# Leaving a root on the residual: post norms that multiply instead of divide, in a fused three-block transformer kernel

## The reference, cut to what matters

```
def rms_norm(x, g):
    y = xf * lax.rsqrt(jnp.mean(xf * xf, axis=-1, keepdims=True) + RMS_EPS)
    return (y * g.astype(jnp.float32)).astype(x.dtype)
...
h = h + rms_norm(mixer(rms_norm(h, mix_pre)), mix_post)
h = h + rms_norm(swiglu_ffn(rms_norm(h, ffn_pre)), ffn_post)
```

## Time and profile before

| | |
|---|---|
| median of 3 runs | 1988.74 us |
| span of the profiled execution (no other time of it is given) | 1988.3 us |
| PE busy | 1601.5 us (81%) |
| DVE busy | 754.2 us (38%) |
| ACT busy | 557.1 us (28%) |
| GpSimd busy | 114.2 us (6%) |
| mean granted TensorE clock | 0.913 |

### The profile page before, as it was taken

One profiled execution on the slowest core, in us unless ns is written; L12 is line 12 of the kernel. 1 busy time (PEld: TensorE's weight loads), 2 busy tenths in 40 slices (PEclk: granted clock), 3 DMA queues, 4 the chain that ended last, 5 costly groups with the idle time before them and its releaser, 6 DMA issues.

```text
span 1988.3 us, 26400 instructions
## 1 busy us (share of the span) xinstructions
PE 1601.5 (81%) x11487; PEld 1134.5 (57%) x11487; DVE 754.2 (38%) x1094; ACT 557.1 (28%) x878; POOL 114.2 (6%) x100
## 2 busy tenths in 40 slices
PE   7999999999899999999999855566555556555556
PEld 7899999998679999897798311111111111111112
DVE  6766767675648555668655100000000000000000
ACT  4454544354754344436653000000000000000001
POOL 1101000000313000003300000000000000000000
PEclk9999999999999999999999988777878777778878
DMA  9854597648165555353278999999999999999997
GB/s 353 300 176 161 136 312 259 225 159 273 57 262 193 194 185 169 127 172 105 86 275 346 420 432 432 432 431 430 431 431 432 431 432 432 431 431 432 429 430 315
DMA packets 100521, 604.31 MB, mean 304 GB/s; under 512 B 5340, under 2 KB 60821, under 8 KB 75336
## 3 DMA queue, kind: packets, MB, share of 16 engines
q1 hardware_dynamic: 91456, 587.22, 73.7%
q10 hardware_dynamic: 7832, 11.26, 1.9%
q0 software_dynamic: 1136, 4.40, 1.6%
HBM read 595.52 MB, written 4.20 MB: 302 GB/s over the span
## 4 chain that ended last, share of the span: by engine, by line
PE 55%; DMA 38%; DVE 4%; ACT 1%; issue 1%; POOL 0%; DVEq 0%; ACTq 0%
DMA _expert_slots_and_tokens<-in_experts 38%; PE ps L772 19%; PE ps L841 13%; PE ps L1469 4%; PE ps L826 3%; PE ps L1288 2%; PE ps L1503 2%; PE ps L794 2%; DVE split_operands L649 1%; PE ps L1051 1%; PE ps L1321 1%; PE ps L1428 1%; PE ps L1311 1%; ACT split_operands L641 1%; PE ps L1064 0%
## 5 line engine op out<-in xcount | busy, mean ns | idle before, releaser
L772 PE MATMUL ps<-split_operands 128*128 128x256 f32 x3360 | 412.2, 284 | 3.1 <-DVE split_operands L649 1.9
L649 DVE TENSOR_TENSOR split_operands<-dense_ring_and_tables,split_operands 128x1024 fp32r<-128x1024 f32 x282 | 343.5, 1260 | 178.5 <-ACT split_operands L641 178.3
L772 PEld LDWEIGHTS ps<-split_operands 128*128 128x128 f32 x3360 | 406.4, 192 | 6.3 <-issue 3.3
L641 ACT ACTIVATE split_operands<-dense_ring_and_tables 128x1024 fp32r<-128x1024 f32 x284 | 284.5, 1050 | 301.8 <-PE ps L772 156.5
L2724 DVE TENSOR_TENSOR arena<-arena,ps 128x512 f32<-128x512 f32 x16 | 11.0, 688 | 570.9 <-PE ps L1469 570.9
L1993 ACT ACTIVATE arena<-ps 128x512 f32<-128x512 f32 x16 | 9.6, 597 | 565.0 <-PE ps L1469 565.0
L841 PE MATMUL ps<-split_operands 128*128 128x256 f32 x1248 | 152.0, 284 | 2.7 <-DVE split_operands L679 2.7
L841 PEld LDWEIGHTS ps<-split_operands 128*128 128x128 f32 x1248 | 150.3, 192 | 4.7 <-DVE split_operands L679 3.5
L841 PE MATMUL ps<-hidden_split,split_operands 128*128 128x256 f32 x960 | 118.6, 283 | 0.8 <-DVE split_operands L649 0.8
L841 PEld LDWEIGHTS ps<-hidden_split,split_operands 128*128 128x128 f32 x960 | 116.6, 192 | 1.0 <-DVE split_operands L649 1.0
L1469 PE MATMUL ps<-_expert_slots_and_tokens,arena 128*32 128x512 f32 x400 | 70.5, 868 | 58.0 <-DMA _expert_slots_and_tokens<-in_experts 58.0
(11 more groups left out here) (361 smaller groups left out, 1781.6 us busy)
## 6 DMA issues: line engine op xcount, KB each, us to landing
dense_ring_and_tables<-in_experts SPq DMA_DIRECT2D x36, 4096.0 KB, 43.2
_expert_slots_and_tokens<-in_experts SPq DMA_DIRECT2D x35, 4096.0 KB, 43.1
arena<-in_experts SPq DMA_DIRECT2D x17, 4096.0 KB, 43.1
dense_ring_and_tables<-in_ffn_units SPq DMA_DIRECT2D x66, 1024.0 KB, 4.9
dense_ring_and_tables<-in_ret_w_in SPq DMA_DIRECT2D x23, 1024.0 KB, 8.1
dense_ring_and_tables<-in_w_in SPq DMA_DIRECT2D x22, 1024.0 KB, 5.1
dense_ring_and_tables<-in_w_ada SPq DMA_DIRECT2D x12, 1024.0 KB, 6.9
arena<-in_experts SPq DMA_DIRECT2D x6, 2048.0 KB, 8.4
```

The lines of the kernel that those rows point to most:

```text
L641: act.activation(w_hi[:, n % 2, c], ring[U % RING][:, c], ACT.Copy).then_inc(hi_ready, 1)
L649: dve.tensor_tensor(w_lo[:, n % 2, c], ring[U % RING][:, c], w_hi[:, n % 2, c], ALU.subtract).then_inc(lo_ready, 1)
L772: mm = pe.matmul(ps[:, bank, b * T:b * T + T], left, right, start=k == 0 and i == 0, stop=k == 7 and i == 2)
```

## The change

- `post`: the residual is left multiplied by the root. DVE makes `xn = h * root` and `h = acc * gain + xn`, so h is root times its true value, and no reciprocal is needed. The next norm's eps must then be multiplied by the square of the root: DVE writes `eps_r2 = root * root * EPS * D / P`, and PE adds ones times `eps_r2` to the sum of squares (`AFTER_POST`). This norm's root is written straight into `rs`.
- `over_root` gives h back its value later: a reciprocal of the root and one product over all of h. It is called in each FFN after `hidden_and_split(1)`, after `kv_out(3)`, and after the split of U_V in the third block's mixer.
- In `post` ACT squares the last two chunks one by one, ahead of the quarter splits. DVE makes the first quarter of `w_hi` itself. All four joints now split in quarters, and GpSimd no longer splits `U_IN2 + 1`.
- `warm` is gone at the first two joints.
- `norm(N_IN2)` sums added squares; `mod_norm` makes gain, shift and remainder chunk by chunk; `wide_tok` takes chunks in the outer loop and token halves in the inner.
- A few counters are merged (`kd2_in`, `moe_root`, `scaled`).

```diff
@@ norm
+                if n in AFTER_POST:
+                    pe.wait_ge(eps_ready, AFTER_POST[n] + 1)
+                    pe.matmul(ps[:, SUM_BANK[n], 0:T], ones[:], eps_r2, start=True, stop=False)
...
+                        if q and n in POST_NO:
+                            pe.wait_ge(*((sq_ready, 4 * n + 4) if c == 7 else (sq_half, POST_NO[n] + 1)))
@@ wide_tok
-                for t in range(2):
-                    for k in range(4):
+                for k, t in ((k, t) for k in range(4) for t in range(2)):
@@ after norm(N_POST0), after norm(N_POSTF0)
-            warm(10, 1, 0)
-            warm(14, 1, 0)
@@ act post
-                for q in range(4):
-                    if q < 3:
-                        act.wait_ge(acc_done, TOLD[n] + q + 1)
-                    else:
-                        taken(act, last)
-                        if n in JOINTS:
-                            quarter_hi_split(act, U + 1, 0)
+                for q in range(3):
+                    act.wait_ge(acc_done, TOLD[n] + q + 1)
...
+                taken(act, last)
+                for c in (6, 7):
+                    act.activation(sq[:, c, :], acc_chunk(ACC[n], c), ACT.Square).then_inc((sq_half, sq_ready)[c % 2], 1)
+                quarter_hi_split(act, U + 1, 1)
                 roots(n)
+                for i in (2, 3):
+                    quarter_hi_split(act, U + 1, i)
@@ dve
+            def over_root(n):
+
+                finished(dve.reciprocal(rs_post, root[:]))
+                dve.tensor_tensor(h, h, rs_post.unsqueeze(1).to_broadcast([P, DC, T]), ALU.mult).then_inc(h_true, 1)
@@ dve post
+                dve.wait_ge(landed[(U + 1) % RING], 16 * ((U + 1) // RING + 1))
+                taken(dve, SPLIT_UNITS[SPLIT_NO[U + 1] - 2])
+                finished(dve.tensor_copy(w_hi[:, SPLIT_NO[U + 1] % 2, 0:UNIT // 4], ring[(U + 1) % RING][:, 0:UNIT // 4]))
+                for i in (0, 1):
+                    quarter_lo_split(dve, n, i)
+                dve.wait_ge(root_ready, n + 1)
+                if POST_NO[n]:
+                    dve.wait_ge(h_true, POST_NO[n])
                 for k in range(10 if next_name else 9):
                     if k < 8:
-                        dve.scalar_tensor_tensor(out=xn[:, k, :], in0=acc_chunk(ACC[n], k), scalar=col(name, k),
-                                                 in1=rs[:], op0=ALU.mult, op1=ALU.mult).then_inc(scaled, 1)
+                        steps[0] += 1
+                        dve.tensor_tensor(xn[:, k, :], h[:, k, :], root[:], ALU.mult).then_inc(dve_step, 1)
                     if 1 <= k < 9:
-                        dve.wait_ge(scaled, POST[n] + k)
-                        dve.tensor_tensor(h[:, k - 1, :], h[:, k - 1, :], xn[:, k - 1, :],
-                                          ALU.add).then_inc(h_ready, 1)
+                        dve.wait_ge(dve_step, steps[0] - (k < 8))
+                        dve.scalar_tensor_tensor(out=h[:, k - 1, :], in0=acc_chunk(ACC[n], k - 1), scalar=col(name, k - 1),
+                                                 in1=xn[:, k - 1, :], op0=ALU.mult, op1=ALU.add).then_inc(h_ready, 1)
...
+                dve.scalar_tensor_tensor(out=eps_r2, in0=root[:], scalar=EPS * D / P, in1=root[:], op0=ALU.mult,
+                                         op1=ALU.mult).then_inc(eps_ready, 1)
@@ ffn, after hidden_and_split(1) / after kv_out(3) / after split_lo(U_V)
+                over_root((N_POST0, N_POST1)[f])
+            over_root(N_POSTF0)
+            over_root(N_POSTF1)
@@ mod_norm
-                for k in range(8):
-                    dve.scalar_tensor_tensor(out=dst[:, k, :], in0=src[:, k, :], scalar=gain[:, i, k:k + 1],
-                                             in1=rs[:], op0=ALU.mult, op1=ALU.mult).then_inc(mod_scaled, 1)
-                shift(dst, row, o)
+                for k in range(11):
+                    if k < 8:
+                        dve.scalar_tensor_tensor(...)
+                    if 1 <= k < 9:
+                        dve.wait_ge(mod_scaled, k)
+                        dve.tensor_scalar(...)
+                    if k >= 3:
+                        token_lo(dve, x0, dst, k - 3)
@@ pool
-            split_lo(pool, U_IN2 + 1)
```

## The result

| | before | changed |
|---|---|---|
| median | 1990.68 us (1988.40 to 1993.59, 12 runs) | 1994.07 us (1992.68 to 1997.39, 12 runs) |
| ratio to before | | 1.0017, 95% interval 1.0010 to 1.0024 |
| profiled execution: time, span | span 1988.3 us | 1995.40 us, span 1993.6 us |
| mean granted TensorE clock | 0.913 | 0.906 |
| DVE busy | 754.2 us | 765.5 us |

The changed kernel is slower by 3.4 us. The forecast was 0.9 us faster, and the widest range of the prediction ended at one fall of the clock, 1991.4. The time lies above it, so the prediction was wrong, in sign and in size. (The ratio itself, 1.0017, is still within the 0.2% that the prediction called the same; its interval reaches beyond.)

What follows compares the result with a forecast made beforehand. Bound: a dense part paced by PE, then a tail paced by transfers. Gains 7.4 less costs 5.3 is 2.1 us faster, less 1.2 for the clock, 0.9: 1987.8 us. Own range 1985.5 to 1989.5; widest from 1983.0 to 1991.4.

Steps and rivals of the forecast that it cites:

- PE's fills go. They hid nothing.: First joint, repeated at the second: taking out PE's fill products was counted as costing nothing.
- the fills were worth their place: Rival: without fills the clock falls at the first two joints, 3.6 us each; chance of both 0.06, of one 0.06.
- Gain 2.2 us ... so 2.2 again: First and second joint: faster squares 0.36 and the reciprocal off the path 1.8, 2.2 us gained at each.
- The second FFN: Restoration there delays gate and splits: PE's wait grows from 0.77 to 4.3 us, cost 3.56, plus 1.2 for the clock.
- The first rival (absorbed, 0.2): The second FFN's restoration is absorbed and costs nothing: 5.7 us faster, 1983.0; chance 0.2.
- Eps's products, 0.7: New eps product ahead of the sum of squares after the first three joints: 0.2 + 0.27 + 0.25, 0.7 us cost.
- Joint 3, 0.9: Third joint (N_POST1): PE, not DVE, is late next, so 0.36 + 0.50 = 0.9 us gained, not 2.2.
- Joint 4, 2.1: Fourth joint (N_POSTF1): without GpSimd's split DVE runs undisturbed, PE reaches the mixer's first product 2.1 us earlier.
- The mixer's restoration, 1.0: Second mixer: restoration ahead of bn_stats delays the split of U_UA, so PE waits 1.0 us.
- The first FFN: Restoration there is hidden by PE's products, with 0.3 us to spare.
- The third rival (ACT late with x_hi): ACT's two quarter splits behind the root make x_hi late: the three joints give 2 less, 1990; chance 0.08.
- The reference: Base of the forecast: the profiled execution's span of 1988.3 us, taken as 0.4 below the median of 1988.74.

Runs made afterwards that it cites:

- run 6: The kernel before with its fills at the first two joints left out: 1995.62 us, ratio 1.0023 to before.
- run 9: The changed kernel with three fill products at the first joint and seven at the second: 1990.24 us, ratio 0.9997 to before.
- Run 1: The changed kernel with the second FFN's restoration moved behind its loop: 1987.89 us, ratio 0.9985 to before.
- run 5: The kernel before with the remainder of U_IN2+1 made by DVE behind the norm N_POSTF1 instead of by GpSimd: 1990.04 us, ratio 0.9994.
- run 10: The changed kernel with the restoration in the third block's mixer moved behind the gating: 1991.56 us, ratio 1.0004 to before.
- run 3: The changed kernel with ACT's copy of the gain rows ahead of the split of U_NQ: 1991.32 us, ratio 1.0003 to before.

## Why the prediction was wrong, point by point

- **The step that failed: "PE's fills go. They hid nothing."** Nothing of the arithmetic hung on them, but they kept the clock. The rival that said so (the fills were worth their place) had chances of 0.06 and 0.06. Its price, 3.6 us for each joint, was too high: a fall costs 1.4 to 1.5 us of the pair here, 2.5 in the kernel before, whose waits without fills are longer. But its chance was far too low. Over the seven profiles of changed kernels without fills at a joint, the first lost clock in three (wait 0.79); over six, the second in five (wait 1.73). I had held two rows against it. The 1.02 us of waiting without a fall stands between dense products, and there no profile shows a fall; it says nothing of a wait behind the short products of a joint. The 2.3 us idle of 5 is one draw: at the same place eight of the twelve profiles have a slow stretch. The same wait after the same work is followed by a fall in one execution and not in the next. Runs 6 and 9 decide it: about 5 us lost without fills in the old kernel, about 4 us regained by them in the new. The Trainium skill ("TensorE: Matmul & The Clock Gate", section "HAM oscillation — how this bites in real kernels") prices longer idle gaps than these, and I let that weigh against the rival. Here gaps of 0.8 and 1.7 us were followed by a fall, and the measurement decides.
- **"Gain 2.2 us ... so 2.2 again":** the two joints measured 2.21 and 2.22, by the steps named. What failed is that they go to the end one for one. I never looked for what is late next behind the second joint: U_NQ. In the kernel before, the rows that stand behind its split on ACT were out at 467.07, and PE came for them at 467.51: 0.4 us to spare, where I was about to bring PE 4 us forward. With the fall in the pair it costs 3.9 us up to L1044, and behind its wait of 1.78 stands another fall (1.1). The KV unit's restoration, which I did check there, is hidden (it ends at 457.1, DVE then waits for a DMA to 458.6).
- **The second FFN:** the mechanism was right and the size near. (The new wait is not longer than any in the dense part, as I wrote: PE idles 9.8 us ahead of its very first product.) Forecast 3.56 + 1.2, measured 3.96 + 1.1. The term was too small by 0.4: the 0.5 I took off, for a split that had waited for ACT, came back in the split that GpSimd now met earlier (5.92 us instead of 5.34). The first rival (absorbed, 0.2) fell. Run 1 shows that it is the placement that costs: the same restoration behind the loop is free.
- **Eps's products, 0.7:** measured 0.0. PE waited there for a weight remainder, and the product fits into that wait: from L749 to L758 it is 0.43 us, and from L758 to L782 it is 0.92 where the kernel before had 1.36. I had charged it 0.51 and let it stick out by 0.2 to 0.27.
- **Joint 3, 0.9:** 1.1. **Joint 4, 2.1:** 2.5, of it 2.0 by the quiet GpSimd (run 5), as argued. These 2.0 need no change of the norm: with the reciprocal in place and GpSimd quiet PE has no wait there (run 5). **The mixer's restoration, 1.0:** 1.0, of it 0.78 as idle time (run 10). **The first FFN:** hidden, as forecast: counted from the pair's start the split comes 1.8 us later (39.1 instead of 37.4), and PE still has no gap. The third rival (ACT late with x_hi) fell: ACT ends its quarters at 224.7 and PE waits for DVE.
- **The reference:** I set the profiled execution at 0.4 below the median of three, which compares a span with a device time. The device time is 1.8 to 2.1 us more than the span in all runs, so that execution took some 1990.2. And 12 to 33 executions of before have their median at 1990.3 to 1990.7. So 1.9 us of the 6.3 between the forecast and 1994.07 are the small sample, and 4.3 are the kernel. In the two profiles the sum is 6.2 off (+5.3 against -0.9): 5.0 behind joint 2, less 1.6 given back, 3.5 in the last part, where the slow stretches differ by execution, and -0.7 of small terms.

**Open:** what makes one execution lose the clock behind the same wait and another not, and so how much of the 4.5 us behind the wide products belongs to the median. Also what makes U_NQ's transfer scatter by 1.5 us when nothing ahead of it differs.

## What to carry to other kernels

Products that compute nothing can be what keeps the clock; before they are taken out, the wait that remains must be near nothing, since 0.8 us was already too much in some executions here; a single trace in which such a wait costs nothing does not show that it is free. Work that is moved off a chain costs nothing only where its engine has room: the same 4 us restoration was free in one FFN and cost 5 in the other, until it went behind the loop. After a gain, walk the path behind it to the first transfer whose wait is nearly as long as the gain, and look who stands behind it in the same queue: one swap of two ScalarE steps took PE's wait of 1.78 us away and the median was 2.75 us lower (run 3).

## What the runs showed of the hardware

- PE waits of 0.79 us and 1.73 us were followed by some 3 us at 1.2 GHz in three of seven and five of six profiles; 11.76 us of products then take 13.20 to 13.28. Behind waits of 2.64 and 3.58 us the slow stretch was some 7 us (0.51 over 7 us, 0.57 over 8) and they took 14.2 to 14.3. Fills of 0.9 and 1.8 us of products of ones in the waits: none in the profiles that had them (two at the first joint, three at the second). The waits of 0.77 and 1.02 us in the second FFN, in the middle of dense products, had no fall in any of the six profiles that show them alone. One fall (run 6, 0.66 in 471 to 476) stands behind a wait of only 0.19 us, after 32 products of 48 columns.
- Beside GpSimd's operations DVE's splits of 128x1024 took 2.7 to 3.0 us each instead of 1.18, and one 128x256 addition 2.1 instead of 0.33; with GpSimd quiet no such row is left (run 5).
- On DVE a cast of 128x512 took 0.43 us, less than the 0.65 I took; a 128x2048 product 2.29 and a reciprocal of 128x256 1.74, the same in each of the restoration's four places.
